# First norm's squares added on VectorE, Fourier steps folded over the tokens, and the expert list made in parts

## What is computed

```
# first block: modulation from silu(c) @ w_ada, then
h = rms_norm(x, g_norm1) * (1 + scale1) + shift1      # mean over the 1024 features
... attention, projection, x = x + gate1 * ...
... h2, router, 64 experts of which 8 a token, shared expert, x = x + gate2 * y
# second model, layer 0, for the tokens and for the context alike:
u, v, g_a, x_b, g_b = split(h @ w_in)
xb = x_b.reshape(bsz, L, 4, 128)                      # L = 256 tokens, 4 groups of 128 channels
f = real(fft2(xb, axes=(1, 3), norm='ortho'))         # over the tokens and the channels
y = concat([y_a, f * silu(g_b)]) @ w_out
# layer 1: window attention over tokens and context, final norm
```

## Time and profile before

| | us |
|---|---|
| median of 3 runs | 1126.29 |
| lowest, highest | 1125.88, 1126.87 |
| the profiled execution | 1125.17 |
| its span, first to last instruction | 1123.4 |
| TensorE busy | 1079.4 (96%) |
| VectorE, ScalarE, GpSimdE busy | 380.8, 277.2, 52.6 |
| mean granted clock | 0.992 |

### The profile page before, as it was taken

One profiled execution on the slowest core, in us unless ns is written; L12 is line 12 of the kernel. 1 busy time (PEld: TensorE's weight loads), 2 busy tenths in 40 slices (PEclk: granted clock), 3 DMA queues, 4 the chain that ended last, 5 costly groups with the idle time before them and its releaser, 6 DMA issues.

```text
span 1123.4 us, 17394 instructions
## 1 busy us (share of the span) xinstructions
PE 1079.4 (96%) x7070; PEld 746.9 (66%) x7070; DVE 380.8 (34%) x974; ACT 277.2 (25%) x619; POOL 52.6 (5%) x85
## 2 busy tenths in 40 slices
PE   6999999999999899999999999999989999999988
PEld 4786776688756465565556655456458888887567
DVE  1298976432722211112111121211332011342941
ACT  2124135501511112112111111102322111212951
POOL 0000202103000000000000000001000001100001
PEclk9999999999999899999999999999999999999999
DMA  9999387945679999999999999999995334210000
GB/s 385 336 421 421 125 346 317 419 186 188 263 311 385 372 422 420 420 408 422 422 419 422 419 422 421 417 422 418 401 410 216 113 113 151 111 38 1 1 1 38
DMA packets 48560, 335.48 MB, mean 299 GB/s; under 512 B 5440, under 2 KB 6816, under 8 KB 8672
## 3 DMA queue, kind: packets, MB, share of 16 engines
q1 hardware_dynamic: 46080, 329.01, 71.9%
q10 hardware_dynamic: 2176, 3.37, 1.0%
q0 software_dynamic: 224, 1.97, 0.4%
HBM read 333.28 MB, written 1.05 MB: 298 GB/s over the span
## 4 chain that ended last, share of the span: by engine, by line
PE 85%; DMA 7%; DVE 5%; ACT 1%; issue 1%; SPq 0%; DVEq 0%; ACTq 0%
PE bank L1068 13%; PE bank L533 12%; DMA ring<-experts 6%; PE bank L1112 6%; PE bank L1019 5%; PE bank L1208 5%; PE bank L919 5%; PE bank L940 3%; PE bank L450 3%; PE bank L975 3%; PE bank L1300 2%; PE bank L825 2%; PE bank L1258 2%; PE bank L840 2%; PE bank L663 2%; PE bank L599 2%
## 5 line engine op out<-in xcount | busy, mean ns | idle before, releaser
L1068 PE MATMUL bank<-ring,arena 128*32 128x512 f32 (+1 forms) x1120 | 175.4, 599 | 5.2 <-DMA ring<-experts 5.1
L533 PE MATMUL bank<-hT,ring 128*128 128x256 f32 x608 | 134.0, 380 | 0.7 <-ACT hT L1494 0.7
L533 PEld LDWEIGHTS bank<-hT,ring 128*128 128x128 f32 x608 | 114.7, 190 | 20.3 <-issue 5.1
L1068 PEld LDWEIGHTS bank<-ring,arena 128*32 128x32 f32 (+1 forms) x1120 | 50.9, 121 | 111.5 <-issue 111.2
L1112 PE MATMUL bank<-ring,arena 128*32 128x512 f32 (+1 forms) x560 | 87.5, 596 | 2.0 <-DMA ring<-experts 1.0
L919 PEld LDWEIGHTS bank<-arena 128*128 128x128 bf16 x1152 | 66.3, 98 | 13.1 <-issue 10.1
L919 PE MATMUL bank<-arena 128*128 128x128 bf16 x1152 | 72.3, 219 | 2.0 <-ACT arena L1660 2.0
L2288 DVE TENSOR_TENSOR yhalf<-bank,yhalf 128x512 fp32r<-128x512 f32 x48 | 33.2, 692 | 93.3 <-ACT yhalf L1697 93.3
L1431 POOL TENSOR_TENSOR hT<-hT 128x256 f32<-128x256 f32 x30 | 21.7, 724 | 842.1 <-ACT hT L1488 840.7
L2275 DVE SCALAR_TENSOR_TENSOR arena<-bank,arena 128x256 f32<-128x256 f32 x24 | 11.6, 484 | 142.3 <-ACT arena L1689 137.7
L1208 PE MATMUL bank<-hT,ring 128*128 128x256 f32 x256 | 56.9, 379 | 0.0
(11 more groups left out here) (379 smaller groups left out, 1443.5 us busy)
## 6 DMA issues: line engine op xcount, KB each, us to landing
ring<-experts SPq DMA_DIRECT2D x188, 1024.0 KB, 13.4
ring<-stream SPq DMA_DIRECT2D x119, 1024.0 KB, 12.2
ring<-experts SPq DMA_DIRECT2D x8, 512.0 KB, 7.7
arena<-consts POOLq DMA_DIRECT2D x1, 1664.0 KB, 12.7
resid<-x SPq DMA_DIRECT2D x1, 1024.0 KB, 5.2
resid<-ctx ACTq DMA_DIRECT2D x1, 1024.0 KB, 10.0
arena<-stream SPq DMA_DIRECT2D x1, 1024.0 KB, 10.1
bias_room<-rpb ACTq DMA_DIRECT2D x2, 438.0 KB, 5.9
```

The lines of the kernel that those rows point to most:

```text
L533: mm = mmul(o[:, 0:n_tok], w[:, k, t * P:(t + 1) * P], hT[:, k, 0:n_tok], start=(k == 0), stop=(k == KT - 1))
L1068: mm = mmul(o[at:at + n_slots, :], xg[:, kk, at:at + n_slots], w[g][:, k, :], start=(kk == 0), stop=(kk == KT - 1))
```

## The change

1. **First norm.** TensorE's eight matmuls of ones go. VectorE adds the eight tiles of squares into tile 0, one add each as it comes; TensorE does one matmul of ones, behind modulation slab 0 and ahead of slab 4.
2. **Folded Fourier step**, for context and tokens. VectorE's `fold_tokens` makes of a z tile x of 256 tokens the sums x[t] + x[256-t] and the differences x[t] - x[256-t] for t in 1 to 127, with x[0] ahead of the sums and x[128] in the place of the first difference. The step over channels is then 128 sums against cosine (128 columns), 128 differences against sine, and one row, that of x[128], against cosine, written over the first row of the sine half. The step over tokens is two matmuls, against 128 rows of cosine and 128 of sine whose first row is cosine of token 128. Tables, copies and buffers shrink to half; `const2` is 256 KB smaller. VectorE's folds stand where the context's z tiles are copied, and for the tokens after v's norm.
3. **The list in parts.** `list_more` is cut in four: after units 1, 2, 3 and 4.
4. **Behind the experts.** Half of the context's keys (k 0 to 3 of tile 0) stand ahead of the last scatter, the other half behind; the four transposed groups come in the order 0, 2, 1, 3.
5. The semaphores for second halves are made when asked for.

The diff, cut to its core:

```
             pe.wait_ge(S("ones_set"), 1)
-            rms_sums("sum1", 0, 256, squared="sq1")
...
             ada_slab("ada1", 0)
+            pe.wait_ge(S("sq1_sum"), KT - 1)
+            close_group(mmul(open_group("sum1", 0)[:, 0:T], ones[:], hT[:, 0, 0:T], start=True, stop=True), "sum1")
             ada_slab("ada1", 4)
...
+            def channels(o, n):
+                mmul(o[:, 0:P], folds[:, n % 2, 0:P], cc("dft_c", 0, P), start=True, stop=True)
+                mmul(o[:, P:2 * P], folds[:, n % 2, P:2 * P], cc("dft_c", P, 2 * P), start=True, stop=True)
+                return mmul(o[0:1, P:2 * P], folds[:, n % 2, P:P + 1], cc("dft_c", 0, P), start=True, stop=True)
+            def tokens(o, at):
+                mmul(o[:, 0:T], at[:, 0:P], cc("dft_l", 0, T), start=True, stop=False)
+                return mmul(o[:, 0:T], at[:, P:2 * P], cc("dft_l", T, 2 * T), start=False, stop=True)
...
-                    done(pe, ("zc", i))
-                    for t in range(TT):
-                        mm = mmul(o[:, 256 * t:256 * t + 256], z_c(i)[:, P * t:P * t + P], cc("dft_c"), start=True, stop=True)
+                    pe.wait_ge(S("folded_c"), i + 1)
+                    mm = channels(o, i)
...
-            scatter(LAST, last=True)
...
-            context_keys(0, 4)
-            for g in range(4):
+            context_keys(0, 4, range(0, 4))
+            scatter(LAST, last=True)
+            context_keys(0, 4, range(4, KT))
+            for g in (0, 2, 1, 3):
...
             def over_channels(g):
-                done(pe, ("z", g))
+                pe.wait_ge(S("folded"), g + 1)
...
+            for k in range(1, KT):
+                dve.wait_ge(S("sq1"), k + 1)
+                if k > 1:
+                    dve.wait_ge(S("sq1_sum"), k - 1)
+                v.tensor_tensor(hT[:, 0, 0:T], hT[:, 0, 0:T], hT[:, k, 0:T], ALU.add).then_inc(S("sq1_sum"), 1)
             mean("n1", "sum1")
...
+            def fold_tokens(src, n, tag):
+                to = folds[:, n % 2, :]
+                back = bass.AP(src.tensor, src.offset + 255, [list(src.ap[0]), [-1, P - 1]])
+                v.tensor_copy(bc(to[:, 0:1], [P, 2]), bc(src[:, 0:1], [P, 2]))
+                v.tensor_tensor(to[:, 1:P], src[:, 1:P], back, ALU.add)
+                v.tensor_tensor(to[:, P + 1:2 * P], src[:, 1:P], back, ALU.subtract).then_inc(S(tag), 1)
...
             for m in range(LAST + 1):
                 unit(m)
-                if m == 1:
-                    list_more()
+                list_more(m - 1)
...
-            for g in range(4):
+            for g in (0, 2, 1, 3):
                 t, hf = g // 2, g % 2
```

More of the change, by code:

```diff
@@ L236, in fa_c @@
         def fa_c(n):
[L237 removed]
+            return hT[:, n % 2, 0:T]
+        folds = ar(6992, 512, 2, 256)
         def z_c(i):
```

107 lines of the change are left out of this document (58 added, 49 removed).

## The result

The change is faster, by less than forecast. Four runs beside the kernel before gave a median of 1118.78 us (1115.88 to 1120.82) against 1126.09, ratio 0.9936, interval 0.9919 to 0.9952. Six more runs gave 1117.41 against 1125.67, ratio 0.9925, interval 0.9911 to 0.9940. The forecast was 1112.8, its range 1109.8 to 1118.5: the median fell 0.3 us outside. "Faster by over 0.2%" came true.

What follows compares the result with a forecast made beforehand. TensorE bounds the kernel ahead of and behind the experts, DMA among them. Savings of 2.4 + 2.7 + 4.2 + 3.6 = 12.9 us gave 1112.3 from the profiled execution; forecast 1112.8 us, range 1109.8 to 1118.5.

Steps and rivals of the forecast that it cites:

- the forecast's 0.67 and 0.86: Latent mixer: the new channel step takes 0.67 us and the new token step 0.86, so 2.59 becomes 1.53.
- Part 1, 2.4 us: First norm: sum ready at 11.3 instead of 13.37, first input matmul near 16.0; 2.4 us saved, ends 0.5 and 2.9.
- Part 2: Context's Fourier step among the experts: worth nothing by itself, since its savings lie where DMA is the bound.
- Part 3, 2.7 us: List after unit 1: TensorE's 6.8 us stall goes, but only the DMA gap counts; 2.7 us, ends 0 and 4.
- Rival 2: Among the experts: DMA's gap does not close, or opens elsewhere; saving 10.2 us, 1115.5 us, chance 0.1.
- The prediction's own sign, the last expert slab 5 us earlier: End of the experts: the prediction is wrong if the last expert slab does not land 5 us earlier than before.
- Part 4, 4.2 us: Latent Fourier step: channel plus token step falls from 2.59 to 1.53 us, times 4, saving 4.2 us.
- Rival 3: Latent mixer: weight loads pace the folded channel step, 0.96 us instead of 0.67; latent gives 3.0, 1114.0 us, chance 0.05.
- Part 5, 3.6 us: Behind the last unit: keys' split gives 1.0 us, the third norm's sum 2.6; 3.6 in all, ends 1.5 and 4.2.
- Rival 1: Third norm's sum: the clock falls ahead of it after all, and the start gives 2.0; 1114.6 us, chance 0.17.
- Rival 5: Expert units: TensorE's slab waits of 4 us and more each drop the clock; slower, 1146 us, chance 0.03.
- the prediction's argument from seven waits without a fall: Experts, 390 to 735 us: seven waits for slabs, the longest 1.3 us, left the granted clock at 1.00.

Runs made afterwards that it cites:

- part 1 alone: Kernel before with the first norm's squares added on VectorE (seven adds) and one summing matmul: 1126.98 us against 1125.21, ratio 1.0008.
- Without part 1, with its fillers (12 and 6): The change with the old eight-matmul sum, plus unread matmuls of ones, 12 ahead of that sum and 6 behind the fold: 1115.49 us, ratio 0.9916.
- padded change: The change with 7 matmuls of ones by ones as TensorE's first work, restoring the instruction count: 1116.36 us against 1125.73, ratio 0.9916.

## Why a Fourier group takes 1.82 us

```
-                mmul(o[:, P:2 * P], folds[:, n % 2, P:2 * P], cc("dft_c", P, 2 * P), start=True, stop=True)
-                return mmul(o[0:1, P:2 * P], folds[:, n % 2, P:P + 1], cc("dft_c", 0, P), start=True, stop=True)
+                return mmul(o[:, P:2 * P], folds[:, n % 2, P:2 * P], cc("dft_c", P, 2 * P), start=True, stop=True)
```

> The change without the third matmul of the channel step (the row of x[128] against cosine is left out, so the first row of the sine half holds x[128] against sine). In the change a channel step takes 0.84 us and the token step behind it 0.97, its first matmul 0.54 where it takes 0.43 with no channel step ahead. Theory A (a load of a full tile of weights can't run beside the matmul of one column, so the row costs its 0.31 and makes its neighbour dearer): channel 0.44 to 0.53, token 0.86, a group about 1.33, latent 1.9 us shorter than the change's 64.08. Theory B (each 128-column matmul is paced by its two loads, 0.3 us, the row no exception): channel 0.55 to 0.6, token 0.97, 1.1 us shorter.

```
-                return mmul(o[0:1, P:2 * P], folds[:, n % 2, P:P + 1], cc("dft_c", 0, P), start=True, stop=True)
+                return mmul(o[:, P:2 * P], folds[:, n % 2, P:2 * P], cc("dft_c", 0, P), start=True, stop=True)
```

> The change with the third channel matmul made with all 128 columns of weights (it overwrites the whole sine half, so the sine products are lost). Theory A (the one-column weights are what disturbs the loads around them): three equal matmuls at 0.22 to 0.28, channel 0.67 to 0.84, and the token step behind it back at 0.86, a group 1.55 to 1.65: 0.5 to 1.0 us shorter over the four groups. Theory B (loads set the pace whatever their width): a group at 1.8 or dearer, no gain.

```
-                mmul(o[:, 0:P], folds[:, n % 2, 0:P], cc("dft_c", 0, P), start=True, stop=True)
                 mmul(o[:, P:2 * P], folds[:, n % 2, P:2 * P], cc("dft_c", P, 2 * P), start=True, stop=True)
                 mmul(o[0:1, P:2 * P], folds[:, n % 2, P:P + 1], cc("dft_c", 0, P), start=True, stop=True)
+                return mmul(o[:, 0:P], folds[:, n % 2, 0:P], cc("dft_c", 0, P), start=True, stop=True)
```

> The change with the channel step's matmuls in the order sine, row, cosine. Theory A (the load behind the row can't run ahead of time): the late load is now that of the cosine matmul, whose stream is shorter, and the token step goes back to 0.86; the group stays within 0.1 of 1.81. Theory B (what costs is the first token matmul being behind a short one): 0.1 us less a group.

The first leaves the row out of the result, the second the sine products; they are there for their times. The mixer took 62.07 us without the row, 62.96 with the wide row, 64.08 with the row in the middle, where the change has 64.08. The timeline of a group without the row, then with the wide one, then (with weight loads, PEld) the row in the middle:

```profile
876.67 0.39 PE L988 MATMUL bank<-arena 128*128 128x128 f32 x2
876.89 0.39 PE L989 MATMUL bank<-arena 128*128 128x128 f32 x2
877.12 0.60 PE L993 MATMUL bank<-arena 128*128 128x256 f32 x2
877.55 0.59 PE L994 MATMUL bank<-arena 128*128 128x256 f32 x2
```

```profile
877.56 0.38 PE L988 MATMUL bank<-arena 128*128 128x128 f32 x2
877.78 0.39 PE L989 MATMUL bank<-arena 128*128 128x128 f32 x2
878.00 0.39 PE L990 MATMUL bank<-arena 128*128 128x128 f32 x2
878.23 0.60 PE L994 MATMUL bank<-arena 128*128 128x256 f32 x2
878.66 0.59 PE L995 MATMUL bank<-arena 128*128 128x256 f32 x2
```

```profile
879.74 0.38 PE L988 MATMUL bank<-arena 128*128 128x128 f32 x2
...
880.05 0.09 PEld L989 LDWEIGHTS bank<-arena 128*1 128x1 f32 x2
880.05 0.38 PE L989 MATMUL bank<-arena 128*1 128x128 f32 x2
880.36 0.30 PEld L990 LDWEIGHTS bank<-arena 128*128 128x128 f32 x2 [0.22 <-issue]
880.36 0.49 PE L990 MATMUL bank<-arena 128*128 128x128 f32 x2
```

With full tiles of weights the spacing is 0.22, 0.22, 0.23 and 0.43, 0.43: exactly the forecast's 0.67 and 0.86. The row with one column of weights is the cheapest to load (0.09 us) and the dearest to have. A full tile's load starts together with the matmul pass ahead of it; the row's load starts 0.20 us behind that start, so from L988 to L989 it is 0.31 us instead of 0.22. The full load behind the row starts 0.20 us behind the row's last pass in the same way (880.36), so the row takes 0.31 too, and the two passes of the matmul behind it stand 0.21 us apart instead of 0.11. Theory A in all three runs, the wide row with 1.12 us a little above its 0.5 to 1.0. Together the row's narrow tile costs 0.28 us a group, 1.12 in all.

## The tail's two edits

The change with the transposed groups in their old order (`for g in range(4)` in both places), the keys split:

> The change with the four transposed groups in their old order 0, 1, 2, 3, the split of the keys kept. From the last down product to the first matmul behind the third norm the change takes 34.43 us and the kernel before 38.38, of which the change's keys should be 1.0 and its order 1.05 plus the higher clock 1.4 by the forecast. Theory A (forecast): the idle ahead of the sum grows to 2.5 us, the clock may fall: 1.0 to 1.1 slower than the change with the clock up, 2.4 to 2.8 with a low stretch near 830. Theory B (the clock is a matter of the moment and not of the order): no low stretch, 1.0 slower.

Its timeline, and below it the window with the clock:

```profile
832.31 5.29 PE L498 MATMUL bank<-hT,ones 128*128 128x256 f32 x16 [2.52 <-ACT hT L1495]
```

```profile
829.00:839.00 10.00, 7.48 (x32) 6.24 (x31) 4.69 (x19) 2.97 (x9) 0.00 (x0) 0.83 1.01 421
```

Idle 2.52 us again and a sum of 5.29 with a low stretch: 2.32 us more than the change from the last down product to the next stage, 1.04 from the order and 1.28 from the clock. The keys gave 1.5 in the profiled pair, by the starts of the last down product and of the transposes. Theory A. But the same two views of the kernel with part 1 alone, which has the old order too:

```profile
834.03 3.69 PE L496 MATMUL bank<-hT,ones 128*128 128x256 f32 x16 [2.52 <-ACT hT L1492]
```

```profile
829.00:839.00 10.00, 7.48 (x43) 6.58 (x42) 5.04 (x20) 2.98 (x9) 0.00 (x0) 1.00 1.02 425
```

The same 2.52 us of idle, and no fall. The old order fell in four profiled executions of five, the new one in none of eleven. The idle was 2.52 us in all five and 1.48 in all eleven. So the order gives 1.04 us always, and some 1.3 more where the old order would have fallen.

## A version that beats both

Without part 1, with its fillers (12 and 6), and with the row made by a full tile of weights: `late` is zero but for x[128] in its first column.

```
-                mmul(o[:, P:2 * P], folds[:, n % 2, P:2 * P], cc("dft_c", P, 2 * P), start=True, stop=True)
-                return mmul(o[0:1, P:2 * P], folds[:, n % 2, P:P + 1], cc("dft_c", 0, P), start=True, stop=True)
+                mmul(o[:, P:2 * P], folds[:, n % 2, P:2 * P], cc("dft_c", P, 2 * P), start=True, stop=False)
+                return mmul(o[:, P:2 * P], late[:, n % 2, :], cc("dft_c", 0, P), start=False, stop=True)
...
+                v.tensor_copy(late[:, n % 2, 0:1], src[:, P:P + 1])
+                v.memset(to[:, P:P + 1], 0.0)
```

> The change without part 1, with the fillers ahead of the sum of squares and behind the fold, and with the row of x[128] made by a full tile of weights: a tile that is zero but for x[128] in its first column, added to the sine half, whose own first column of weights is zero. The product is the same. Theory A (one-column weights cost what the run with wide weights gave back): a group of the latent mixer at 1.54 instead of 1.81, the mixer 1.1 us shorter at 62.96, 1114 to 1115. Theory B (adding into the sine half, or VectorE's two more small steps, cost as much): mixer at 64.1, 1115.5.

Measured: 1112.89 (5 runs, 1112.12 to 1116.31) against 1125.73, ratio 0.9895, interval 0.9880 to 0.9910; the mixer 62.96 us. Faster than the kernel before by 1.05%; the change itself, on another chip, has 0.75%, its interval beginning at 0.9911, so the two just miss each other; on its own chip its interval overlaps that of the padded change (0.9903 to 0.9930).

```profile
871.18 0.38 PE L995 MATMUL bank<-arena 128*128 128x128 f32 x2
871.40 0.39 PE L996 MATMUL bank<-arena 128*128 128x128 f32 x2
871.62 0.39 PE L997 MATMUL bank<-arena 128*128 128x128 f32 x2
871.85 0.60 PE L1001 MATMUL bank<-arena 128*128 128x256 f32 x2
872.28 0.59 PE L1002 MATMUL bank<-arena 128*128 128x256 f32 x2
```

## Why the runs of the change differ by 5 us

The second profiled execution of the change ended 3.3 us after the first. It was 0.9 us ahead at the fixed matmul, and 2.1 behind at unit 0. The two places between, in the first execution and in the second:

```profile
140.00:155.00 15.00, 14.99 (x69) 10.53 (x68) 6.84 (x13) 9.29 (x12) 0.00 (x0) 0.89 1.01 419
174.00:186.00 12.00, 10.81 (x134) 6.55 (x132) 9.01 (x39) 8.12 (x24) 7.04 (x11) 1.00 0.90 354
```

```profile
140.00:155.00 15.00, 15.00 (x63) 9.80 (x62) 5.21 (x11) 8.97 (x12) 0.00 (x0) 0.77 0.98 400
174.00:186.00 12.00, 10.81 (x106) 6.24 (x108) 6.99 (x30) 6.54 (x20) 5.25 (x8) 0.86 0.77 283
```

Behind the 32 matmuls of L803, which have one column of input each, the clock falls in every execution, but for twice as long in ten of the sixteen profiled executions, which costs 1.44 us (the mean over 140 to 155 is 0.77, not 0.89); near 178, where TensorE waits, it falls in five of sixteen, 1.63 us. Neither place is touched by the change. The first profiled execution of the change had the short form of the first and none of the second, so its 9.6 us flatter the change, and the medians' 7.3 and 8.3 are the better figure.

## Why the prediction was wrong, point by point

- **What bounds the kernel**: right. The Fourier step among the experts was worth nothing, that in the mixer all it saved on TensorE, and the list only DMA's gap.
- **Part 1, 2.4 us: wrong; the step that failed the forecast.** It gave about 0.2 at the start (0.5 in the profiled pair) and nothing by the medians of part 1 alone. In the change it also cost 1.9 us of the expert stream on average, by its count of instructions, a term that the prediction did not have. The step "most of them ran at 1.2 GHz: 0.86 us each instead of 0.43" took one execution's 6.45 us for the kernel's; five executions of the same code run from 5.13 to 6.59. "I expect the same stretch at 1.2 GHz, a few tenths sooner" supposed that the first work, 1.8 us later and with waits in it, leaves the clock as it was; the low stretch was 3.4 us in some executions, 6.8 in the profiled one and 13.7 in the padded one. The sum was ready at 11.98 in the profile, where the prediction had 11.3. The lower end of 0.5 was too high: no row excluded a loss.
- **Part 2**: right, nothing (506.55 against 506.49).
- **Part 3, 2.7 us**: the mechanism was right, and so was the size: 3.2 alone. The over 10 us of waits for slabs came (14.1), and TensorE was 8.4 us ahead at unit 3 and 4.4 at unit 4. In the change about 1.9 us of it was lost again behind slab 153. Rival 2 named this ("an instruction fetch") but as a gap of the list's; what brought it was part 1's count of instructions. The prediction's own sign, the last expert slab 5 us earlier, follows from its 2.4 + 2.7 and fails with them: that slab came 3.0 us earlier in one execution and 0.3 later in the other (822.01).
- **Part 4, 4.2 us**: 3.1. The mis-sized term is "three matmuls at 0.22": with full weights it is 0.67 and 0.86 to the hundredth, and the one-column row adds 0.28 a group. Rival 3 gave the right size, 3.0, for another reason: loads of 128 columns did not set the pace, the neighbours of the small one did. The rule of the Trainium skill cited there (Back-to-back issue gap) asked for dearer full matmuls; the wide run's 0.22 speaks against it here.
- **Part 5, 3.6 us**: 3.95 in two traces. Keys 1.5 instead of 1.0 (their slab was there, so the scatter slipped less), order 1.04 as forecast, clock 1.4 in the pair. Rival 1 did not happen in any of eleven executions.
- **Rival 5**: its mechanism exists, without its price. In the run without the row, a wait of 3.5 us for a slab was followed by 5.34 us for 32 records instead of 3.64. Unit 4 then starts 3.3 us later than in the change, and slab 110 had landed 3.3 us later too, from delays ahead of unit 0: while DMA is the bound, the half rate cost nothing there. Two more executions fell like this, behind waits for slabs of 3.04 and 1.94 us (wide row) and of 2.60 (old order, keys split), while the change's wait of 2.82 us at 382 was not followed by a fall. So the prediction's argument from seven waits without a fall, the longest 1.3, did not carry to longer ones.
- **The range**: its top, 1118.5, was drawn by rival 1. Its forecast stands between the sum taken off the profiled execution (1112.3) and off the median (1113.4). It lacked the case that part 1 gives nothing, and took the profiled execution as 1.1 us from the median, where executions of one kernel spread 1 to 7 us over places that the change doesn't touch.
- **The sum again**, by the traces: 0.2 for part 1, 3.2 for the list, 3.1 for the Fourier step and 3.95 for the tail make 10.45; less the 1.9 of the expert stream 8.6, where the medians say 7.3 and 8.3. The size of the miss comes from part 1 (4.1 us with the stream) and part 4 (1.1).

What stays open: whether the change is slower or faster with part 1 than without. By traces it should be 1.7 us slower (1.9 in the stream less 0.2 at the start); the medians, 1117.41 with and 1118.25 without, say neither. Open too is why the count of instructions costs behind slab 153 and not ahead of it, and why part 1 alone has the highest median of all.

## What to carry to other kernels

Read a duration in a stage of cold clock from more than one execution before you count on its removal; and ask not only which work goes, but what the engine will have done by the time its next work comes. Keep weight tiles full: a row made with one column of weights cost more than one made with 128, most of them zero. When a stream of transfers is the bound, removing instructions from a long program can also shift it, and a pad of the same count tells that from the edit itself. Compare such streams at several points: at slab 94 the change looked 1.4 us behind, and at slab 101 it was not.

## What the runs showed of the hardware

- A one-column weight tile loads in 0.09 us, but its load starts 0.20 us behind the start of the pass ahead, and so does that of the full tile behind it, where a full tile's load between full ones starts with that pass: 0.28 us for each such matmul between full ones.
- Slabs land 1.2 to 1.5 us late at a handful of places in 187, mostly with a 16 KB packet of the instruction queue 2 to 6 us ahead. Slabs 90, 94, 142 and 154 are late in both executions of the change; with seven more matmuls at the start it is 100 and 146 instead.
- At the start the granted clock of a window reads 1.00 over 7 to 13 us, while eight f32 matmuls of 256 columns take up to 6.59 us instead of 3.45: the column doesn't show the slow matmuls there. Durations do.
- Idle of the same length at the same place (2.52 us) was followed by the lower clock in four executions and not in a fifth. Among the experts, waits of 3.53, 3.04, 2.60 and 1.94 us were followed by it, one of 2.82 was not.
